# Attention heads of a fused four-mixer kernel: another order of exponentials, evictions, projections and weight splits

## What is computed

```python
def mla_attention(q_nope, q_rope, k_nope, k_rope, v):
    def block(args):                       # 128 queries
        qn_i, qr_i, i = args
        sc = jnp.einsum('bqhd,bkhd->bhqk', qn_i, k_nope) + jnp.einsum('bqhr,bkr->bhqk', qr_i, k_rope)
        sc = sc.astype(jnp.float32) * scale
        q_chunk = (i * Q_BLOCK + jnp.arange(Q_BLOCK)) // CHUNK
        mask = k_chunk[None, :] <= q_chunk[:, None]
        sc = jnp.where(mask[None, None], sc, -jnp.inf)
        p = jax.nn.softmax(sc, axis=-1).astype(v.dtype)
        return jnp.einsum('bhqk,bkhd->bqhd', p, v)
...
    y = (jax.nn.silu(gate) * o) @ w_out
```

## Time and profile before

| | us |
|---|---|
| median of three runs | 2762.57 (2758.68 to 2766.36) |
| the profiled execution | 2753.27 |
| its span, first to last instruction | 2751.5 |
| TensorE busy in it | 2600.8 (95%) |
| VectorE, ScalarE, GpSimd busy | 1151.9, 864.2, 421.5 |
| the eight heads, first S0 to last store | 1116.1 to 1389.0 |
| mean granted clock of TensorE | 0.977 |

### The profile page before, as it was taken

One profiled execution on the slowest core, in us unless ns is written; L12 is line 12 of the kernel. 1 busy time (PEld: TensorE's weight loads), 2 busy tenths in 40 slices (PEclk: granted clock), 3 DMA queues, 4 the chain that ended last, 5 costly groups with the idle time before them and its releaser, 6 DMA issues. The chain is left out here.

```text
span 2751.5 us, 36261 instructions
## 1 busy us (share of the span) xinstructions
PE 2600.8 (95%) x13200; PEld 2200.9 (80%) x13200; DVE 1151.9 (42%) x2217; ACT 864.2 (31%) x1567; POOL 421.5 (15%) x891
## 2 busy tenths in 40 slices
PE   8999999997897999999878999997989999999998
PEld 7888888886686987777757788886768888888887
DVE  4333333323322420577744577655433333333333
ACT  5322222222212422554433444433232221122112
POOL 4444444442000204000001011101000000000000
PEclk9999999999998999999989999998989999999999
DMA  6211111102432221211143211101432111111111
GB/s 234 67 46 59 48 59 48 54 19 87 147 107 79 90 89 52 56 56 56 47 142 118 66 37 34 58 25 48 164 124 96 54 38 46 50 57 46 41 51 69
DMA packets 73822, 196.75 MB, mean 72 GB/s; under 512 B 8128, under 2 KB 29568, under 8 KB 72832
## 3 DMA queue, kind: packets, MB, share of 16 engines
q1 hardware_dynamic: 73728, 195.50, 21.8%
HBM read 153.53 MB, written 37.75 MB: 70 GB/s over the span
## 5 line engine op out<-in xcount | busy, mean ns | idle before, releaser
L542 PE MATMUL ra_qkv_ps<-ra_wh,ra_xl 128*128 (+1 forms) x512 | 206.6, 403 | 11.8 <-DVE ra_wl L489 9.4
L2542 PE MATMUL ff_f_ps<-x_upper,ff_w1l 128*128 128x512 f32 x512 | 201.1, 393 | 6.4 <-DVE ff_w1l L2478 6.4
L542 PE MATMUL ra_qkv_ps<-ra_wh,ra_xh 128*128 (+1 forms) x512 | 200.9, 392 | 0.0
L2542 PE MATMUL ff_f_ps<-x_lower,ff_w1h 128*128 128x512 f32 x512 | 200.6, 392 | 0.0
L2542 PE MATMUL ff_f_ps<-x_upper,ff_w1h 128*128 128x512 f32 x512 | 200.6, 392 | 0.0
L542 PE MATMUL ra_qkv_ps<-ra_wl,ra_xh 128*128 (+1 forms) x512 | 200.4, 391 | 0.0
L2555 PE MATMUL ff_y_ps<-ff_w2h,ff_hl 128*128 128x512 f32 x512 | 199.2, 389 | 0.0
L2555 PE MATMUL ff_y_ps<-ff_w2l,ff_hh 128*128 128x512 f32 x512 | 199.2, 389 | 0.0
L2555 PE MATMUL ff_y_ps<-ff_w2h,ff_hh 128*128 128x512 f32 x512 | 199.2, 389 | 0.0
L2505 DVE TENSOR_TENSOR ff_acc<-ff_y_ps,ff_acc 128x1024 f32<-128x1024 f32 x64 | 78.4, 1225 | 213.9 <-PE ff_y_ps L2555 213.9
L2446 ACT ACTIVATE ff_relu<-ff_f_ps 128x512 f32<-128x512 f32 x64 | 38.3, 598 | 379.2 <-PE ff_f_ps L2542 379.2
(11 more groups left out here) (392 smaller groups left out, 6493.1 us busy)
## 6 DMA issues: line engine op xcount, KB each, us to landing
staging<-in_w_ff SPq DMA_DIRECT2D x64, 512.0 KB, 3.9
ra_raw<-in_w_in_a SPq DMA_DIRECT2D x30, 768.0 KB, 4.6
gated_a<-ra_sg SPq DMA_DIRECT2D x64, 128.0 KB, 1.9
staging<-in_w_out_a SPq DMA_DIRECT2D x16, 512.0 KB, 3.6
staging<-in_w_vr_c SPq DMA_DIRECT2D x16, 512.0 KB, 4.1
wa_gin<-gated_a SPq DMA_DIRECT2D x6, 1024.0 KB, 4.8
staging<-in_x_cols SPq DMA_DIRECT2D x8, 512.0 KB, 5.0
ra_opening<-in_x SPq DMA_DIRECT2D x8, 512.0 KB, 7.9
```

The source lines that it names most:

```text
L542: last = pe.matmul(out, a[:, kt, t * P:(t + 1) * P], b[:, ds(slot, 1), kt, at:at + n].rearrange("p a n -> p (a n)"), start=(kt == 0 and i ...
L2542: last = pe.matmul(f_ps[j % 2][:, :], a[:, kt, f * P:(f + 1) * P], b[:, kt, half * HALF:(half + 1) * HALF], start=(kt == 0 and i == 0), st ...
```

## The change

Only the heads are reordered; the same products, exponentials, copies and DMAs are done. On TensorE T7 of the head before moves behind S1, and J1 moves in front of V3. On ScalarE and VectorE: the exponential (normalisation) of odd blocks and of block 0 comes before the eviction of the transposes of the block before; the split of v moves from block 6 to block 1; the weights' split is cut in two, pieces 2, 3, 4 behind block 2 and pieces 0, 1 behind block 4, where all five stood behind block 5; and the lower halves of T7 stand behind the maximum of S1. The semaphores of the weights count two steps per head, and each part waits for the projections that read its pieces.

```diff
             def load_weights(h):
-                sp.wait_ge(wl_done, h)
+                sp.wait_ge(wl_done, 2 * h)
...
-            def w_upper(h, first=False):
-                act.wait_ge(w_in, 16 * h + 16)
+            def w_upper(h, part, first=False):
+                if part == 0:
+                    act.wait_ge(w_in, 16 * h + 16)
                 if not first:
-                    act.wait_ge(j_mm, 4 * h)
-                for k in range(5):
+                    act.wait_ge(j_mm, 4 * h - 2 + 2 * part)
+                for k in ((2, 3, 4), (0, 1))[part]:
...
             def head(h, u, first, behind):
                 for i in range(NT):
-                    if i:
+                    if i == 1 and not first:
+                        transposed_upper(h - 1, NT - 1)
+                    if i and i % 2 == 0:
                         transposed_upper(h, i - 1)
                     exponential(h, i, i if first else 2)
-                    if i == 0 and not first:
-                        transposed_upper(h - 1, NT - 1)
+                    if i == 1 and behind:
+                        project_upper(h + 1, 1 - u, i)
+                    if i % 2:
+                        transposed_upper(h, i - 1)
+                    if i in (0, 2, 3) and behind:
+                        project_upper(h + 1, 1 - u, i)
                     if i == 0:
                         r_upper(h, 1)
                     if not behind:
                         continue
-                    if i < 4:
-                        project_upper(h + 1, 1 - u, i)
+                    if i == 1:
+                        v_upper(h + 1, 1 - u)
+                    if i in (2, 4) and behind > 1:
+                        w_upper(h + 2, i // 2 - 1)
                     if i == 5:
                         r_upper(h + 1, 0)
-                    if i == 6:
-                        if not first:
-                            act.wait_ge(v_mm, 4 * h)
-                        v_upper(h + 1, 1 - u)
-                    if i == 5 and behind > 1:
-                        w_upper(h + 2)
...
             def head(h, u, first, behind):
                 for i in range(NT):
-                    if i:
-                        maximum(h, i)
-                        if i >= 3 and i % 2:
-                            gate(h, (i - 3) // 2, u)
-                        if i == 1 and not first:
-                            gate(h - 1, 3, 1 - u)
+                    maximum(h, i)
+                    if i == 1 and not first:
+                        transposed_lower(h - 1, NT - 1)
+                    if i and i % 2 == 0:
                         transposed_lower(h, i - 1)
-                    else:
-                        maximum(h, 0)
-                        if not first:
-                            transposed_lower(h - 1, NT - 1)
                     normalise(h, i)
+                    if i == 1 and behind:
+                        project_lower(h + 1, 1 - u, i)
+                    if i == 1 and not first:
+                        gate(h - 1, 3, 1 - u)
+                    if i >= 3 and i % 2:
+                        gate(h, (i - 3) // 2, u)
+                    if i % 2:
+                        transposed_lower(h, i - 1)
+                    if i in (0, 2, 3) and behind:
+                        project_lower(h + 1, 1 - u, i)
                     if i == 0:
                         r_lower(h, 1)
                     if not behind:
                         continue
-                    if i < 4:
-                        project_lower(h + 1, 1 - u, i)
+                    if i == 1:
+                        v_lower(h + 1, 1 - u)
+                    if i in (2, 4) and behind > 1:
+                        w_lower(h + 2, i // 2 - 1)
                     if i == 5:
                         r_lower(h + 1, 0)
-                    if i == 5 and behind > 1:
-                        w_lower(h + 2)
-                    if i == 6:
-                        v_lower(h + 1, 1 - u)
...
             def project(h, g, first=False):
 
-                if g == 0:
-                    pe.wait_ge(wl_done, h + 1)
+                if g % 2 == 0:
+                    pe.wait_ge(wl_done, 2 * h + g // 2 + 1)
...
                     if i == 0 and behind:
                         project(h + 1, 0)
-                    if i == 0 and not first:
+                    if i == 1 and not first:
                         transposes(h - 1, NT - 1, 2)
+                    if i == 1 and behind:
+                        project(h + 1, 1)
                     if i == 1 and not first:
                         values(h - 1, 3, 1 - u)
...
-                    if 0 < i < 4 and behind:
+                    if 1 < i < 4 and behind:
                         project(h + 1, i)
```

More of the change, by code:

```diff
@@ L1551, in _ @@
             r_copy(2)
-            w_upper(0, True)
+            w_upper(0, 0, True)
+            w_upper(0, 1, True)
             for t in range(NT):
@@ L1563, in _ @@
             r_upper(0, 0)
-            w_upper(1)
+            w_upper(1, 0)
+            w_upper(1, 1)
             act.wait_ge(v_copied, NT)
@@ L1599, in _, with w_lower @@
         def _(dve):
-            def w_lower(h):
-                dve.wait_ge(wh_done, h + 1)
-                for k in range(5):
+            def w_lower(h, part):
+                dve.wait_ge(wh_done, 2 * h + part + 1)
+                for k in ((2, 3, 4), (0, 1))[part]:
                     last = dve.scalar_tensor_tensor(wl[:, k, :], raw[:, k, :], gains[:, k:k + 1],
@@ L1673, in head @@
                         continue
-                    if i < 4:
-                        project_lower(h + 1, 1 - u, i)
+                    if i == 1:
+                        v_lower(h + 1, 1 - u)
+                    if i in (2, 4) and behind > 1:
+                        w_lower(h + 2, i // 2 - 1)
                     if i == 5:
                         r_lower(h + 1, 0)
-                    if i == 5 and behind > 1:
-                        w_lower(h + 2)
-                    if i == 6:
-                        v_lower(h + 1, 1 - u)
-            w_lower(0)
+            w_lower(0, 0)
+            w_lower(0, 1)
             for g in range(4):
@@ L1686, in _ @@
             r_lower(0, 0)
-            w_lower(1)
+            w_lower(1, 0)
+            w_lower(1, 1)
             v_lower(0, 0)
```

## The result

| us | before | after |
|---|---|---|
| median | 2760.62 (2756.82 to 2766.36, four runs) | 2741.98 (2739.28 to 2742.88, four runs) |
| ratio | | 0.9926, interval 0.9912 to 0.9940 |
| profiled execution, its span | 2753.27, 2751.5 | 2742.34, 2740.5 |
| second comparison, median | 2760.77 (2753.10 to 2763.34, 17 runs) | 2742.85 (2738.49 to 2746.39, six runs) |
| its ratio | | 0.9949, interval 0.9933 to 0.9964 |

The kernel is faster by 0.5 to 0.7%, some 14 to 20 us; the forecast was 9.3 us and a range that ended at 2744. The direction was right, and the size too small.

A forecast was written before the change was run, and what follows sets the result against it. TensorE, busy 95% of the span, was taken as the bound, with 30.8 us of waits the most to win. 6.5 + 1.1 + 0.8 + 0.9 = 9.3 us off the median 2762.57 gave 2753.3, range 2744 to 2762.

The forecast's parts named there:

- 6.5 + 1.1: Gains in us forecast for the inner heads: 6.5 for five periods at 1.3 each, 1.1 for the last but one head.
- The walk of the inner head: One steady inner head timed instruction by instruction on all engines in the new order; claimed 32.4 us for 33.7.
- c: Stretch of an inner head from its first to its third score block; forecast 9.8 us for 11.05, a gain of 1.25.
- Rival 1: VectorE's chain from third score block to sixth block's transposes is longer than walked; 3 to 4 us won, 2759; chance 0.17.
- part a: Stretch of an inner head from third score block to sixth block's transposes; forecast 16.7 us for 15.4, a loss of 1.3.
- I take that it falls as before: Assumption that TensorE's clock still falls after the waits at the first head, where it was 0.50 during the first projection.
- 0.8 for the first head: Gain in us forecast for the first head, including 0.54 less wait before its first projection.
- 0.9 for the last: Gain in us forecast for the last head, where no projections cover the moved transposes, with slow clock after its waits.
- Rival 2: Waits go and the clock stays up in first head's first projection and last head's last value products; 12 to 18 us, 2748; chance 0.12.
- 1.4 for the weights: Gain per inner head from sixth block's transposes to the next head's first score block, by moved weight pieces: 5.9 us for 7.3.
- 1.25 for TensorE's row: Gain in us per inner head between first and third score block, from the moved transposes and projection.

## Why the prediction was right, and where not

The sum, by its own terms, as the mean of the two profiles of each kernel:

| us | forecast | before | after | won |
|---|---|---|---|---|
| six periods, second head's S0 to last head's S0 | 6.5 + 1.1 | 200.88 | 191.65 | 9.23 |
| first head | 0.8 | 32.3 | 30.3 | 2.0 |
| last head, S0 to the start of V3's last matmul | 0.9 | 39.7 | 36.9 | 2.8 |
| the stage | 9.3 | | | 14.05 |

**The walk of the inner head held.** Stretch by stretch it was right to 0.2 us (table above). As forecast, neither V2, V3 nor T7 waits in the inner head, T5 has its longest wait, 1.03 us, ended by the lower half of T4, and TensorE's waits in the stage are 18.9 us (21 forecast). V1 waits 0.25 where the text had 0.5. J1 doesn't wait in the third head, and ScalarE's upper halves of the weights wait for no DMA: in the timeline of the kernel after the weights' load is issued at 1187.81 and they start at 1195.24 straight behind J2's upper half. The forecast was still 1.6 us too small over these six periods, some 0.25 each, the part of a (0.17), of c (0.07) and the rounding that the forecast took on the low side.

**Rival 1 fell.** Back-to-back pairs of VectorE keep the 0.08 that they start early: the normalisation of 0.62 at 1205.73 is followed at 1206.27, 0.54 after it, and T5, which ends the chain of part a, started 0.17 before the walk. The page "VectorE: DVE Perf Modes" of the Trainium skill, section "The DRAIN you can't avoid", has the next operation wait until the pipe is empty, and then excepts one that the engine does not hold back, which starts earlier. The trace agrees with the exception, by these 0.54 for 0.62.

**What went wrong is the edges with the clock.** The step was "I take that it falls as before", with 0.8 for the first head and 0.9 for the last, where 2.0 and 2.8 were measured. Taken at equal clock the two terms were right: with 3.4 us at the lower level the first head took 31.88 before (second profile) and 30.98 after (second profile), 0.9 less; with 3.4 us in each, the last head from S0 to the start of its own V3 took 34.36 before and 33.32 after, 1.0 less. The other 3 us go with less time at the lower level. The first heads had 6.8 and 3.4 us of it before and 0 and 3.4 after; the last heads had 6.8 and about 13 us before, 6.8 and 3.4 after.

That the two terms came out so well was in part luck. For J0 the forecast had 0.54 us less wait; it was 1.20, and J0 started 0.89 us after S0 for 2.00. Part of that went into a wait of 0.82 before J1, which the forecast didn't have (0.55 in the second profile). And 0.9 for the last head doesn't follow from what stands beside it: 2.27 less 4.0, with 1.6 won, is about -0.1.

T7 and V3 in the last head of the kernel after:

```profile
1342.63 1.06 PE L1752 MATMUL at_T_ps<-ident,at_prob 128*128 128x128 f32 x8 [0.70 <-DVE gate_lower L1641]
1346.46 0.39 PE L1707 MATMUL at_v_ps<-gate_upper,gate_lower 128*128 128x256 f32 x1 [2.77 <-DVE gate_lower L1641]
```

T7 waits 0.70 for 2.27, and V3 behind it 2.77, for the forecast's 1.0 and 3. The clock fell during V3 in both profiles of the kernel after. In the kernel before it fell at T7 in one (six matmuls in 1.46 us) and at V3 in the other, where T7's eight took 1.09 behind the same 2.27.

Rival 2, with a chance of 0.12, had 3 us for a clock that stays up, and with them the forecast's two edges, 0.8 + 0.9 + 3 = 4.7, meet the measured 4.8. But only half of its condition came true: J0 of the first head ran at the full level in one profile of two, and this V3 in neither. It had some 2.4 of its 3 us in the first head, where 1.2 were measured beyond the forecast, and 0.8 in the last, where it was 1.9. So its sum met the measured one by luck. What the forecast had wrong is that it took one execution's clock as fixed. The runs show it as a draw: it fell at the first J0 in one of two profiles of the same kernel after. The page "TensorE: Matmul & The Clock Gate" of the Trainium skill, section "Why this matters for your kernels", wants no long idle gaps between bursts of matmuls, and means longer ones than the 2.10 us here. In these runs the clock fell behind gaps of 2.10 us and 1.20 us with six matmuls between them, and the same gap of 2.10 stands before S0 in the execution in which it stayed up and in the one in which it fell, so no rule on the gap alone fits.

**Median against profile.** The forecast took 9.3 us off the median of the runs. The stage accounts for 14.05 us of the gain, 0.51% of the whole. The second comparison's ratio agrees, with 0.0051 x 2760.8 = 14.1 us (9.9 to 18.5 by its interval), and so do the fastest runs in it, 2753.1 - 2738.5 = 14.6. The first comparison's ratio gives more, 0.0074 x 2760.6 = 20.4 (16.6 to 24.3), and the medians differ by 18.6 and 17.9. What goes beyond 14, some 4.6 us of the first medians' 18.6, is not in the stage of these profiles; outside it the same kernel differs by 11 us from profile to profile. The forecast put nothing there. With the stage's 14.05 alone it would have been 2748.5, inside the range, so it is this rest that took the measured time 2 us past its end of 2744. Whether the new order has an effect of its own there stays open; no row of the profiles shows one.

**What the change consists of.** The forecast gave each edit a term of its own (1.4 for the weights, 1.25 for TensorE's row, 1.3 lost in part a). The experiments show that they are not terms: TensorE's row alone loses 26 us in the stage (slow clock included), the others' rows alone 5, the weights' place is worth 1.36 per head in the old order and nothing in the new one (-0.16), and the late eviction of odd blocks, which the forecast did not price by itself, loses 0.5 in an inner head. The walk gave the right number for the inner head because it followed all rows together.

## What to carry to other kernels

When engines with rows in fixed order hand work to each other, walk a whole period with all rows at once, and do not add up the gains of single moves; one that wins alone can be worth nothing with the others, and two that win together can each lose alone. Look first for holes that an engine has by necessity (here VectorE between a maximum and its reciprocal, while ScalarE makes the exponential) and put independent work there: 1.1 us per head for two moved calls, as against 1.6 for the whole reordering. And compare a stage by its own time in the trace: two profiles of the same kernel here differ by 11 us outside the stage, nearly as much as the change won inside it.

## What the runs showed of the hardware

The granted clock is not fixed by the program. With the same instructions and the same waits (2.10 us before S0) it stayed at 1.00 over the first J0 in one profile of the kernel after and went to 0.65 over four microseconds in another, and the same 60 us of a later stage had 0.89 and 0.80. The first head of one kernel spent 6.8 us at the lower level in one profile and 3.4 in the next. Nor is it fixed within one execution. With TensorE's old row in the new kernel, V3 waits 2.14 to 2.39 us in seven heads, and the clock fell within 1.5 us of the end of four of these waits. With the new row in the old kernel, J1 waits 3.17 to 3.25 us in six heads, and it fell behind all six. Two executions of one kernel differed by 13 us in a span of 2750, at mean clocks of 0.977 and 0.970, with inner heads that agree to 0.05 us.
